# Up projections of two MLPs by Strassen's seven products in place of eight, in a float32 kernel on one Trainium2 core

## The reference

```python
def sq_relu_mlp(h, w1, w2):                      # w1 1024x4096, w2 4096x1024, all float32
    return jnp.square(jax.nn.relu(h @ w1)) @ w2

# layer 0: 512 latent tokens and 256 context tokens; layer 1: the 512 latent tokens alone
h_lat = h_lat + ml[5] * sq_relu_mlp(modulate(rms_norm(h_lat, norm2_w[layer]), ml[3], ml[4]), mlp_w1[layer], mlp_w2[layer])
if need_ctx:
    h_ctx = h_ctx + mc[5] * sq_relu_mlp(modulate(rms_norm(h_ctx, norm2_w[layer]), mc[3], mc[4]), mlp_w1[layer], mlp_w2[layer])
```

## Time and profile before

| what | us |
| --- | --- |
| median of 3 runs | 2884.98 |
| lowest and highest of them | 2881.59, 2889.4 |
| span of the profiled execution | 2890.5 |
| PE busy in it | 2746.6 (95%) |
| DVE, ACT, POOL busy | 1152.2, 921.4, 400.6 |

### The profile page before, as it was taken

One profiled execution on the slowest core, in us unless ns is written; L12 is line 12 of the kernel. 1 busy time (PEld: TensorE's weight loads), 2 busy tenths in 40 slices (PEclk: granted clock), 3 DMA queues, 4 the chain that ended last, 5 costly groups with the idle time before them and its releaser, 6 DMA issues. The chain is left out here.

```text
span 2890.5 us, 50817 instructions
## 1 busy us (share of the span) xinstructions
PE 2746.6 (95%) x21852; PEld 2073.4 (72%) x21852; DVE 1152.2 (40%) x1696; ACT 921.4 (32%) x1523; POOL 400.6 (14%) x329
## 2 busy tenths in 40 slices
PE   8987989999999999899999999999997888999999
PEld 6764654444445885667888888887786777788887
DVE  3225442323323416644433323234354554544333
ACT  4234331111112224255331212223374545432322
POOL 0014120000000402353100000010004564100001
PEclk9999999999999999999999999999999999999999
DMA  6537819999995112100111211211210000223231
GB/s 252 204 120 278 310 59 372 417 410 418 414 412 204 46 51 61 34 30 30 59 59 58 73 58 62 69 58 59 91 37 31 4 4 33 88 88 98 91 102 58
DMA packets 160787, 390.40 MB, mean 135 GB/s; under 512 B 17007, under 2 KB 108042, under 8 KB 147818
## 3 DMA queue, kind: packets, MB, share of 16 engines
q1 hardware_dynamic: 148378, 199.19, 20.4%
q10 hardware_dynamic: 12240, 188.75, 15.6%
HBM read 381.36 MB, written 5.77 MB: 134 GB/s over the span
## 5 line engine op out<-in xcount | busy, mean ns | idle before, releaser
L2175 PE MATMUL ps<-mlp_h_low,mlp_w_high 128*128 128x512 f32 (+1 forms) x768 | 272.0, 354 | 0.0
L2175 PE MATMUL ps<-mlp_h_high,mlp_w_high 128*128 128x512 f32 (+1 forms) x768 | 271.9, 354 | 0.0
L2175 PE MATMUL ps<-mlp_h_high,mlp_w_low 128*128 128x512 f32 (+1 forms) x768 | 271.6, 354 | 0.0
L2028 ACT ACTIVATE mlp_w_high<-mlp_ring 128x2048 fp32r<-128x2048 f32 x64 | 122.2, 1912 | 316.2 <-PE ps L2175 316.2
L2175 PE MATMUL ps<-mlp_x_low,mlp_w_high 128*128 128x512 f32 (+1 forms) x576 | 204.0, 354 | 0.0
L2175 PE MATMUL ps<-mlp_x_high,mlp_w_high 128*128 128x512 f32 (+1 forms) x576 | 203.9, 354 | 0.0
L2175 PE MATMUL ps<-mlp_x_high,mlp_w_low 128*128 128x512 f32 (+1 forms) x576 | 203.7, 354 | 0.0
L260 POOL TENSOR_TENSOR aT<-aT 128x512 f32<-128x512 f32 (+1 forms) x25 | 52.1, 2084 | 1000.7 <-ACT aT L252 1000.1
L2032 DVE TENSOR_TENSOR mlp_w_low<-mlp_ring,mlp_w_high 128x2048 fp32r<-128x2048 f32 x64 | 146.6, 2292 | 62.8 <-ACT mlp_w_high L2028 62.8
L2244 DVE SCALAR_TENSOR_TENSOR hT<-ps,mod,hT 128x512 f32<-128x512 f32 x96 | 63.5, 662 | 256.0 <-PE ps L2175 256.0
L2175 PEld LDWEIGHTS ps<-mlp_h_high,mlp_w_high 128*128 128x128 f32 x768 | 145.2, 189 | 20.5
(11 more groups left out here) (566 smaller groups left out, 5942.7 us busy)
## 6 DMA issues: line engine op xcount, KB each, us to landing
mlp_ring<-in_mlp_w_dram SPq DMA_DIRECT2D x64, 1024.0 KB, 5.3
e_wg<-in_w_gate_dram ACTq DMA_DIRECT2D x15, 4096.0 KB, 16.2
e_wu<-in_w_up_dram ACTq DMA_DIRECT2D x15, 4096.0 KB, 15.1
ring<-in_w_down_dram ACTq DMA_DIRECT2D x15, 4096.0 KB, 13.2
ring<-in_ada_w_dram SPq DMA_DIRECT2D x16, 2048.0 KB, 8.8
h_rest<-in_ada_w_dram SPq DMA_DIRECT2D x8, 2048.0 KB, 8.2
ring<-in_w_in_dram SPq DMA_DIRECT2D x6, 2048.0 KB, 10.6
proj_ring<-in_even_w_in_dram SPq DMA_DIRECT2D x8, 1024.0 KB, 5.1
```

The source lines that it names most:

```text
L2028: act.activation(self.high[:, slot], self.ring[:, slot], ACT.Copy).then_inc(self.w_high, 1)
L2175: last = pe.matmul(bank(st, n, s, b - a), w[:, st % 2, k, n * P:(n + 1) * P], x[:, k, a:b], start=(k == 0 and p == 0), stop=(k == KT - 1 a ...
```

## The change

`WeightParts` becomes `ProductParts`, `Normed` of the MLPs becomes `NormedBlocks`, and `mlp` becomes `mlp_by_blocks`. The 4096 middle features go in 8 chunks of 512. A chunk has two halves u = 0 and 1 of 256 features. In a half the weight (1024 x 256) is cut into 2 x 2 blocks of 512 x 128, and the activations (1024 x T) into 2 x 2 blocks of 512 x T/2. Seven products of block sums, e = 0 to 6, each 4 (`k`) x 3 matmuls of 128 x T/2, take the place of eight products of blocks. Then come four down steps (`dn`) with four units (`q`) of 4 x 3 matmuls of 128 x T/2.

What is new on the other engines: POOL makes four sums of weight blocks for each half (`combine`); ACT and DVE split seven weight operands of 128 x 512 for each half, and seven activation operands once for each MLP, for which POOL and DVE make differences of activation blocks; ACT copies three products and one sum from PSUM to `E.aT` (`snapshot`), and DVE adds up the four results c11, c12, c22, c21 and squares their positive part. Core of the diff:

```diff
-class WeightParts:
+class ProductParts:
+    NEED = {1: 1, 3: 3, 4: 4, 5: 2}
+    SUM_AT = {1: 0, 5: 1, 4: 2, 3: 3}
+    def combine(self, pool, c, u):
+        z = 2 * c + u
+        first, second, third, fourth = (self.sums[:, i] for i in range(4))
+        pool.wait_ge(self.loaded[u], 16 * (2 * c + 1))
+        pool.tensor_tensor(first, self.block(u, 1, 0), self.block(u, 1, 1), ALU.add).then_inc(self.summed, 1)
+        pool.wait_ge(self.summed, 4 * z + 1)
+        pool.tensor_tensor(second, first, self.block(u, 0, 0), ALU.subtract).then_inc(self.summed, 1)
+        pool.wait_ge(self.summed, 4 * z + 2)
+        pool.tensor_tensor(fourth, self.block(u, 0, 1), second, ALU.subtract).then_inc(self.summed, 1)
+        pool.tensor_tensor(third, self.block(u, 0, 0), self.block(u, 1, 0), ALU.subtract).then_inc(self.summed, 1)
...
+class NormedBlocks(Normed):
+    def highs(self, act):
...
+        shift(0)
+        shift(1)
+        high(0, 0)
+        shift(2)
+        shift(3)
+        high(0, 1)
+        shift(4)
+        high(1, 0)
+        shift(5)
+        high(1, 1)
+        shift(6)
+        shift(7)
+        for e in range(2, 7):
+            for j in range(2):
+                high(e, j)
+    def lows(self, dve):
...
+        for k in range(4):
+            scale(k)
+        low(0, 0)
+        scale(4)
+        scale(5)
+        low(0, 1)
+        scale(6)
+        low(1, 0)
+        scale(7)
+        low(1, 1)
+        low(2, 0)
+        second(0)
+        low(2, 1)
+        second(1)
+        for e in range(3, 7):
+            for j in range(2):
+                low(e, j)
+    def beside(self, pool):
+        for j in range(2):
...
+            pool.tensor_tensor(self.first[:, k:k + 2], self.at(k, 1), self.at(k, 0), ALU.subtract).then_inc(self.t1, 1)
...
+            pool.tensor_tensor(self.at(k, 1), self.at(4 + k, 1), self.at(k, 1), ALU.subtract).then_inc(self.t3, 1)
...
+            pool.wait_ge(self.t2, j + 1)
+            pool.wait_ge(self.x_low, 4 + j + 1)
+            pool.tensor_tensor(self.at(4 + k, 0), self.at(4 + k, 0), self.second[:, k:k + 2], ALU.subtract).then_inc(self.t4, 1)
...
+            @block.tensor
+            def _(pe):
...
+                with pe.Fori(0, C) as c:
+                    for u in range(2):
+                        pe.wait_ge(added, PIECES * (4 * c + 3 + u))
+                        for e in range(7):
+                            pe.wait_ge(W.w_low, 18 * c + 7 * u + e + 1)
+                            if e in (2, 3, 6):
+                                pe.wait_ge(copied, 4 * (2 * c + u) + {2: 1, 3: 2, 6: 4}[e])
...
+                    for dn in range(4):
...
+                        if dn < 2:
+                            pe.wait_ge(made, 4 * (2 * c + dn + 1))
...
+                        for q, (n, half) in enumerate(DOWN):
+                            for k in range(4):
+                                if dn == 0 and q == 0:
+                                    pe.wait_ge(h_low, 8 * c + (3, 4, 6, 7)[k])
+                                if dn == 0 and q == 2 and k == 3:
+                                    pe.wait_ge(h_low, 8 * c + 8)
...
+                        snapshot(c, u, 0, "p1")
+                        weight(0)
+                        snapshot(c, u, 1, "p5")
+                        weight(1)
+                        snapshot(c, u, 2, "c11")
+                        weight(2)
+                        weight(3)
+                        hidden(c, u, "c11", 0)
+                        snapshot(c, u, 4, "p7")
+                        weight(4)
+                        weight(5)
+                        hidden(c, u, "c12", 1)
+                        hidden(c, u, "c22", 2)
+                        weight(6)
+                        hidden(c, u, "c21", 3)
```

More of the change, by code:

```diff
@@ L252, in square, with add @@
         act.activation(self.square_of(self.E, n, self.T), self.E.hT[:, n, 0:self.T], ACT.Square).then_inc(self.squared, 1)
-    def add(self, pool):
+    def add(self, pool, between=None):
         total = self.sum_of(self.E, self.T)
         for n in range(1, KT - 2):
+            if between and n == 4:
+                between(pool)
             pool.wait_ge(self.squared, n + 1)
@@ L698, in _ @@
             def _(pool):
-                squares.add(pool)
+                squares.add(pool, then.get("pool") if then else None)
         if twice:
@@ L2069, in output_and_mlp @@
     with ExitStack() as c1:
-        W = WeightParts(E, c1, f"mlp{layer}", ring)
+        W = ProductParts(E, c1, f"mlp{layer}", ring)
         with ExitStack() as c2:
@@ L2074, in output_and_mlp @@
             resid_gemm(E, f"wout{layer + 2}", w, E.aT, T, lambda n, s: E.mod[:, layer, 16 + n, s:s + 1],
-                       Squares(E, f"wout{layer + 2}", T), fetch, dict(act=W.first_highs, dve=W.first_lows), ahead=ahead)
-        mlp(E, layer, T, W, Squares(E, f"mlp{layer}_end", T), ring, odd_weights(E)[0:2] if follow else [])
+                       Squares(E, f"wout{layer + 2}", T), fetch, dict(act=W.first_highs, dve=W.first_lows, pool=W.first_sums),
+                       ahead=ahead)
+        mlp_by_blocks(E, layer, T, W, Squares(E, f"mlp{layer}_end", T), ring, odd_weights(E)[0:2] if follow else [])
     if follow:
```

420 lines of the change are left out of this document (272 added, 148 removed).

## The result

| | before | after |
|---|---|---|
| median, us | 2886.39 (4 runs, 2881.59 to 2889.4) | 2982.24 (4 runs, 2976.74 to 2989.23) |
| ratio, 95% interval | | 1.034, 1.0309 to 1.0371 |
| profiled execution: span, mean clock | 2890.5, 0.982 | 2987.4, 0.967 |

What follows compares the result with a forecast made beforehand. TensorE's stream of matmuls was taken to bound both MLPs. Terms -37.9 (PE) + 16.8 + 25.7 (heads) + 52 (MLP 1's chunks) + 25 (MLP 0's) gave +82 us, 2967 us on the median; range 2903 to 3010.

Steps and rivals of the forecast that it cites:

- What PE gains, -37.9: Matmuls of both MLPs: fewer columns save 35.2 us in MLP 0 and 2.7 in MLP 1, if PE never waits.
- One line: DVE instructions with two SBUF inputs and POOL's block each other, so their times add: +82 us, against +32 side by side.
- a sign of being wrong: The prediction is wrong if POOL starves less than its one long row of 8073 ns shows.
- (c): Sign: POOL's t4 and sums at several times 1.3 and 1.8 us beside DVE, DVE instructions of 1.5 to 2 us.
- Rival 1: POOL and DVE hardly disturb each other, their instructions stay short: +32 us, 2917 us; chance 0.17.
- Heads, 25.7 and 16.8: First chunks: product 2 waits behind ACT's copy and POOL's t4, 25.7 us late in MLP 0, 16.8 in MLP 1.
- MLP 1's chunks, +52: PE waits 0.6 us at product 6, 2.5 at product 2 of half 1, 3.4 in first down step; times 8.
- rival 2: DVE keeps up and no chunk waits, only the heads remain: -17 us, 2868 us; chance 0.07.
- MLP 0's chunks, +25: PE waits 0.9 and 2.2 us in each chunk of MLP 0, times 8.
- Rival 3, the clock: Long PE waits drop the clock to half, 1.7 us per fall, 21 falls: +36 us, 3003 us; chance 0.16.
- the forecast case, full clock: The main forecast: DVE and POOL as one line, PE at full clock, +82 us; chance 0.60.

Runs made afterwards that it cites:

- e9: e3 with POOL's six differences of the normed activations made by DVE; ratio 1.0206 to the kernel before.
- e1: The changed kernel without any of POOL's sums of weight blocks, output no longer the reference's; ratio 1.0176 to the kernel before.
- e3: The changed kernel with POOL's sums for the next chunk waiting for 18 low parts in place of 13; ratio 1.0211 to the kernel before.
- e5: e3 with down parts 1 and 2 split behind c21 of half 1 on ACT and DVE; ratio 1.0142 to the kernel before.
- e7: e3 with ACT copying half 1's first product ahead of its high part of c21 of half 0; ratio 1.0176 to the kernel before.
- e10: Both MLPs by blocks, joining e3, e5, e6, e7 and e9; ratio 1.0087 to the kernel before.
- e4: The changed kernel with 14 constant products on PE at MLP 0's wait in the first down step; ratio 1.0299 to the kernel before.
- e6: e3 with ACT copying products 1 and 5 of each first chunk ahead of high parts 5 and 6; ratio 1.0208 to the kernel before.
- e12: e11 with POOL's first sums of MLP 0 waiting for all 14 low parts in place of 4; ratio 0.9969 to the kernel before.
- e11: e10 with MLP 1 by the code of before, so blocks in MLP 0 alone; ratio 0.9974 to the kernel before.
- e2: The changed kernel with the sums of weight blocks made by DVE in place of POOL, the first chunk's first sums excepted; ratio 1.0191 to the kernel before.

## Why the prediction was right

The time lay 15 us above it, inside the range. That the sum came so near is in part luck, as the steps show:

- **What PE gains, -37.9.** Right: 0.1736 and 0.120 us. The 173 ns of the estimate stood. (That the weight loads lie beside the matmuls is to be read from the earlier trace rows; the earlier trace rows has matmuls alone.)
- **One line.** The mechanism is shown: DVE's two-SBUF-input instructions and POOL's sums do not run side by side. The rows show the two alternate, so that a turn takes nearly the sum of both (2 x 0.5 us of DVE beside two sums of 1.3 took 3.2). But POOL never starved: its longest instruction in the two MLPs took 2.5 us (768 wide, 1.8 at best), far from the 8.07 of the earlier trace rows. The prediction had named that as a sign of being wrong, and here it was wrong: not that one engine holds the other, but for how long. Of (c), the long DVE instructions came, 2.0 us at 768 beside a sum and 2.6 beside t4; POOL "at several times 1.3" did not. The Trainium skill (SBUF — State Buffer, "Who interferes with whom") speaks of one interface held for a whole instruction; the trace agrees by the 3.18 and 3.16 us, and an alternation is what such a hold would give when both queues are full. Rival 1 would have had these stay short.
- **Heads, 25.7 and 16.8.** The size came out, by luck: the first chunk is 23.2 us longer than the mean of the others in MLP 0 and 17.1 in MLP 1 (91.8 - 68.6, 65.5 - 48.4), and PE starts 3.5 and 2.1 us later, together 26.7 and 19.2. The path was off: product 2 began 27.9 and 18.7 us behind the norm, not 33.3 and 22.1, since t4 was not kept out. The rest came from waits that the step did not have, ahead of later products and in the first down step, and from the clock, which the step had at nothing and which cost some 8 us in each first chunk. POOL's sums for half 1 also fall into the head (1456.52 on); the step had not counted them, and e9's expectation fell by the same omission.
- **MLP 1's chunks, +52.** The waits were at the three places, 0.76, 1.4 and 1.8 us in place of 0.6, 2.5 and 3.4; the chunk 48.4 on average in place of 49.7, that is 5.2 x 8 = +42. The cause was apportioned wrongly: I gave POOL 2.5 of 6.5 us a chunk; e1 takes 1.4 us of waits away with its sums and gives the time back to the clock, e3 changes nothing. e5 and e7 showed the order on DVE and ACT (a down part of 1.23 us ahead of the sum of product 5, which I had named in rival 2, and a copy behind c21) to hold 1.9 us a chunk (46.0 in e10 against 47.9). The 2.8 us that e10 still has over 43.2, 0.76 of them ahead of product 6, no run took apart.
- **MLP 0's chunks, +25.** This is the step that was mis-sized. It was put at 3.1 us a chunk and measured 68.6 - 62.4 = 6.2, x 8 = +50. My walk had 2.2 us in the first down step where 3.75 and 0.8 came, because it did not have POOL's sums for the next chunk fall on the squares and low parts of c12 and c22. e3 shows that as the cause (4.3 to 6.4 us a chunk gone, with one number). Of these the clock was 1.4 to 3.3 us.
- **Rival 3, the clock.** Its price per fall (1.7 us) was right for the short falls, its place was not: I put it in MLP 1's waits of 2.5 and 3.4 us, and it fell behind MLP 0's 2.67 and 3.75 and in both first chunks. e4 measured some 12 us for it in MLP 0, and the granted clock of the profile gives 30 us in both MLPs (16 of them in the first chunks), near the 36 of rival 3. So the forecast case, full clock, is not what happened: the waits were shorter than forecast, and the clock filled the gap.

25 us too little in MLP 0's chunks, 10 too much in MLP 1's, 3 too little in the heads (26.7 and 19.2 measured) and some -3 outside the MLPs make up the 15.

## What to carry to other kernels

A scheme that saves products pays with sums, and here the sums and splits cost more than the products saved. At 256 columns seven products in place of eight saved 2.7 us of 348, because each matmul costs some 13 ns beside its columns at all three widths run here (227, 173.6 and 120 ns for 512, 384 and 256). When work goes to an idle engine, look at which operands it shares a path with and at what moment its trigger (here a transfer's landing) lets it start: the 56 sums for next chunks cost 37 us more started at one moment than started a few us later. All sums left out (e1) gave 10 us more than that, no more than its uncertainty, with 8 us more of clock loss than e3 against it. Before mending one wait, ask which queue is next: in the first chunk of MLP 0 three mendings (e6, e9, e12) moved the wait and none shortened the chunk by more than 0.2 us; with the changes of e5 and e7 beside them it fell from 85.5 to 83.1 (e10) and 81.6 (e11).

## What I had not expected of the hardware

- POOL and DVE with two SBUF inputs share by turns: beside each other, a 768-wide DVE low part takes 1.9 to 2.0 us (0.91 alone) and a 512-wide POOL sum 1.9 to 2.0 (1.29 alone). Evacuations with a PSUM operand are not held: in e3 the 256-wide ones take 476 ns (median of 70) while POOL runs beside them and 483 (of 122) while it doesn't. Why one POOL instruction of the earlier trace rows took 8.07 us no run explains.
- Each wait of 2.67 or 3.75 us in MLP 0's steady chunks was followed by 3.4 or 6.8 us at a granted clock of 0.50. In MLP 1 waits of 0.76, 1.4 and 1.8 us left it at 1.00 in six chunks of seven; in e1 and e2, with 0.9 to 1.0 and 1.83 and shorter waits in sum, it fell in six of seven. What decides it stays open.
